# Three last weight groups walked one token half at a time, norms started before the next splits, modulation sums read first in a step

## The chip, the cores and the metric

The kernel runs on one NeuronCore of a Trainium2 chip. The metric is the time of one launch on the device in microseconds (us), the median of several runs. TensorE (PE) multiplies, VectorE (DVE) and ScalarE (ACT) work elementwise, GpSimd (POOL) does a few tiny powers, SyncE (SP) issues most DMAs. Everything is in fp32, with matrix products made of three products of rounded parts (below).

## The reference

All matrices have 256 tokens (two halves of 128 rows) and D = 2048 features. Cut to what matters here:

```
x = x + rmsnorm(y @ w_o[l], post_norm_g[l])          # end of each of two layers of block one
# block two, once:
sh1, sc1, g1, sh2, sc2, g2 = split(silu(c) @ w_mod + b_mod)   # w_mod is 2048 x 12288, one row vector c
h = rms_norm(x, g0) * (1 + sc1) + sh1
y = real(fft2(h in 8 groups of 256 features)) @ fnet_w_out    # over tokens and features
x = x + g1 * rms_norm(y, n1)
h = rms_norm(x, n2) * (1 + sc2) + sh2
x = x + g2 * rms_norm(square(relu(h @ w_mlp_in)) @ w_mlp_out, n3)
```

A layer of block one is: rmsnorm, one wide projection (latents, keys, a short gated convolution, memory queries, gates), two low-rank up-projections, attention of 8 heads with rotary positions, memory attention of 4 heads, a gate, and the output product with w_o.

## The kernel before

**Steps.** The whole program is a list of 576 steps. A step is half of a 1 MB unit of weights: two or so k-tiles of 128 x 512. SP loads units into a ring of four (`raw`), ACT writes the rounded high part of a step's weights (`split_hi`, L349, into a ring of four `whi`), DVE writes the rest in place (`split_lo`, L356, `wlo`), and PE makes three products per tile: activations high x weights high, high x low, low x high. Eight steps make a group (sixteen for the memory product, two in the up-projections), which fills two or four PSUM banks. Steps 0 to 287 are the two layers (144 each; the last 32 of a layer are w_o in four groups), 288 to 319 the product after the Fourier mix (four groups), 320 to 575 the MLP in four quarters of 64 steps (32 in, 32 out). The last groups of the three stages are thus steps 280 to 287, 312 to 319 and 568 to 575.

**Order.** Every engine walks the same list in its own instruction stream; nothing is reordered. ACT and DVE run `AHEAD = 3` steps ahead: in their iteration s they first split step s+3 and then do whatever else stands at s. `split_hi(s)` waits for the unit and for `half_used >= s-3`, which PE raises at the end of each step. SP loads unit u once unit u-4 is used up.

**w_mod.** The row vector times w_mod is made beside all this on DVE: 192 units of 128 x 1024 (`modacc`, L895), each at a step that a table names; 16 of them make a chunk, after which PE sums over partitions at a step of the same table (`mod_sums`, eight products with ones into one PSUM column, behind a wait for DVE), and DVE adds the eight columns to `modT` (`mod_added`, in the next iteration). Some PE work in that PSUM bank waits for that addition (`sums_read`).

**Ends of stages.** At the end of a stage, before the next one can begin, for both token halves: ACT squares the last group's outputs with a sum over the row (L590), DVE scales them into `otok` (L844), adds the four partial sums (L881), POOL adds eps and takes the power -0.5 (L549, L551), DVE adds to X (`residual`, L870, 2048 wide), ACT squares the new X (L583), POOL again. Then, after the layers, DVE scales the tables of the Fourier mix by the token's factor (`csx`, L1114) and PE multiplies X with them (64 products, all eight banks, here called the AB products) and then mixes within feature groups (64 more). Before the MLP, PE transposes the 16 feature tiles of X (L1439, two per bank) and a tile of the factors (`xrot`, L1450); ACT copies the factors (`mrow`, L806); then for each feature tile DVE multiplies (`x2_value`, L1163), ACT rounds (`x2_round`, L810) and DVE takes the rest (`x2_rest`, L1168): a pair of tiles feeds one MLP step. The first MLP group writes the four banks in which X tiles 0 to 7 lie, and so waits for their eight values. At the end of the MLP the same chain leads to the stores.

**Opening.** ACT waits for the first memory tiles, then loads its function table, rounds memory tiles (L601) and splits weights; DVE makes the rotary angles first (L852 to L860); step 7 waits for a tile made of the memory norm's factors (`mrot`, L1059), and ACT squares X at step 5.

## Time and profile before

| | |
|---|---|
| median of 3 runs | 1779.96 us (1779.45 to 1781.57) |
| the profiled execution | 1779.79 us, its span 1778.0 us |
| busy: PE, DVE, ACT, POOL | 1707.7, 1169.4, 833.7, 22.4 us |
| mean granted TensorE clock | 0.987 |

The span runs from the first to the last instruction. Times in the trace count from the span's start. PEclk is the granted share of TensorE's 2.4 GHz, so that 0.50 is 1.2 GHz.

### The profile page before, as it was taken

The numbers are of one execution on the slowest core, as the hardware profiler recorded it, in microseconds if no ns is written. First come the engines' busy times: TensorE is split into PE (matmuls) and PEld (weight loads), VectorE is DVE, ScalarE is ACT, GpSimd is POOL, SyncE is SP. The second block draws the span as 40 slices with busy tenths as digits, with TensorE's granted clock in tenths as the row PEclk, the third lists the DMA queues.
The fourth block names the chain that finished last, engine by engine and source line by source line (L and its number), as shares of the span: only waits on it lengthen the run. The fifth ranks groups of instructions, "written<-read, shape, count | busy, mean of one in ns | idle before, by whom it ended". The sixth has DMA issues, their size and how long they took to land.

```text
span 1778.0 us, 24585 instructions
## 1 busy us (share of the span) xinstructions
PE 1707.7 (96%) x10182; PEld 1526.7 (86%) x10182; DVE 1169.4 (66%) x1243; ACT 833.7 (47%) x1134; POOL 22.4 (1%) x35
## 2 busy tenths in 40 slices
PE   5999999999999999999979969999999999999997
PEld 5899999988889999998878858888888888888885
DVE  6677756687777866677748868644774455445554
ACT  5556545444655645544444444433443344334442
POOL 0010000000100000000000000000000000000000
PEclk9999999999999999999989989999999999999999
DMA  7587656698667857688837828656875555566553
GB/s 267 180 314 282 238 180 242 219 344 311 213 219 272 316 188 248 208 297 283 302 107 264 318 93 316 193 182 194 298 248 190 189 189 189 190 213 190 189 190 118
DMA packets 184927, 408.29 MB, mean 230 GB/s; under 512 B 8912, under 2 KB 21488, under 8 KB 184048
## 3 DMA queue, kind: packets, MB, share of 16 engines
q1 hardware_dynamic: 183808, 406.40, 66.6%
q8 instruction: 81, 1.33, 0.3%
q10 hardware_dynamic: 1008, 0.32, 0.1%
q14 instruction: 30, 0.25, 0.0%
HBM read 404.58 MB, written 2.11 MB: 229 GB/s over the span
## 4 chain that ended last, share of the span: by engine, by line
PE 89%; DVE 4%; DMA 4%; ACT 1%; issue 1%; POOL 0%; SPq 0%; DVEq 0%; ACTq 0%; POOLq 0%
PE banks L360 88%; DMA modw<-in_w_mod 3%; DVE modacc L895 1%; DVE wlo L356 1%; PE banks L1313 1%; DVE X L870 1%; DMA ropev<-in_rope_c 0%; ACT junk L583 0%; PE banks L1276 0%; ACT whi L349 0%; POOL sc L551 0%; DVE otok L844 0%; ACT junk L590 0%; DVE X L1233 0%; DVE sqr L1211 0%
## 5 line engine op out<-in xcount | busy, mean ns | idle before, releaser
L356 DVE TENSOR_TENSOR wlo<-raw,whi 128x1024 fp32r<-128x1024 f32 (+3 forms) x576 | 682.7, 1191 | 484.7 <-ACT whi L349 483.3
L349 ACT ACTIVATE whi<-raw 128x1024 fp32r<-128x1024 f32 (+3 forms) x576 | 590.5, 1031 | 735.7 <-PE banks L360 693.9
L360 PE MATMUL banks<-H,whi 128*128 128x256 f32 (+1 forms) x3072 | 744.4, 326 | 12.7 <-DVE vtmp L1163 7.7
L360 PE MATMUL banks<-H,wlo 128*128 128x256 f32 x2048 | 579.5, 283 | 0.0
L360 PEld LDWEIGHTS banks<-H,whi 128*128 128x128 f32 x3072 | 516.1, 191 | 63.2 <-DVE vtmp L1163 8.0
L360 PE MATMUL banks<-whi,Y 128*128 128x512 f32 x1536 | 475.6, 390 | 0.0
L360 PEld LDWEIGHTS banks<-H,wlo 128*128 128x128 f32 x2048 | 391.5, 191 | 0.1
L360 PEld LDWEIGHTS banks<-whi,Y 128*128 128x128 f32 x1536 | 288.5, 188 | 59.9
L360 PE MATMUL banks<-wlo,Y 128*128 128x512 f32 x768 | 299.3, 390 | 0.0
L895 DVE SCALAR_TENSOR_TENSOR modacc<-modw,cv,modacc 128x1024 f32<-128x1024 f32 x180 | 230.2, 1279 | 25.2 <-DMA modw<-in_w_mod 24.9
L360 PEld LDWEIGHTS banks<-wlo,Y 128*128 128x128 f32 x768 | 144.3, 188 | 29.5
L360 PE MATMUL banks<-whi,H 128*128 128x512 f32 (+1 forms) x512 | 149.8, 374 | 0.0
L360 PEld LDWEIGHTS banks<-whi,H 128*128 128x128 f32 x512 | 94.8, 190 | 15.0
L360 PE MATMUL banks<-wlo,H 128*128 128x512 f32 (+1 forms) x256 | 95.3, 372 | 0.0
L360 PEld LDWEIGHTS banks<-wlo,H 128*128 128x128 f32 x256 | 48.7, 190 | 7.4
L360 PE MATMUL banks<-memh,whi 128*128 128x256 f32 x128 | 38.2, 298 | 16.5 <-DVE wlo L356 16.5
L724 ACT ACTIVATE prob<-banks,sc 128x256 f32<-128x256 f32 x48 | 22.3, 470 | 55.0 <-DVE sc L1030 55.0
L833 ACT ACTIVATE Y<-sqr 128x1024 fp32r<-128x1024 f32 x16 | 17.0, 1062 | 52.5 <-DVE sqr L1211 52.5
L360 PEld LDWEIGHTS banks<-memh,whi 128*128 128x128 f32 x128 | 25.7, 201 | 17.0 <-issue 16.9
L360 PE MATMUL banks<-memh,wlo 128*128 128x256 f32 x128 | 37.3, 292 | 0.0
L360 PE MATMUL banks<-meml,whi 128*128 128x256 f32 x128 | 37.3, 292 | 0.0
L767 ACT ACTIVATE prob<-prob,sc 128x256 f32<-128x256 f32 x48 | 21.8, 502 | 22.2 <-DVE sc L1034 22.0
(183 smaller groups left out, 1223.3 us busy)
## 6 DMA issues: line engine op xcount, KB each, us to landing
modw<-in_w_mod SPq DMA_DIRECT2D x192, 512.0 KB, 6.2
raw<-in_w_in SPq DMA_DIRECT2D x72, 1024.0 KB, 5.2
raw<-in_w_mlp_in SPq DMA_DIRECT2D x64, 1024.0 KB, 5.2
raw<-in_w_mlp_out SPq DMA_DIRECT2D x64, 1024.0 KB, 5.0
raw<-in_w_o SPq DMA_DIRECT2D x32, 1024.0 KB, 5.3
raw<-in_w_fnet SPq DMA_DIRECT2D x16, 1024.0 KB, 5.2
raw<-in_w_mv SPq DMA_DIRECT2D x8, 1024.0 KB, 5.4
raw<-in_w_mk SPq DMA_DIRECT2D x7, 1024.0 KB, 5.4
```

The lines of the kernel that those rows point to most:

```text
L349: nc.scalar.activation(whi[step % HIR][:, 0:n], raw[u % RAW][:, (step % 2) * n:(step % 2) * n + n], ACT.Copy).then_inc(hi_ready, 1)
L356: nc.vector.tensor_tensor(wlo[u % RAW][:, part], raw[u % RAW][:, part], whi[step % HIR][:, 0:n].bitcast(F32), ALU.subtract).then_inc(lo_re ...
L360: return nc.tensor.matmul(o, a, b, start=start, stop=stop, skip_group_check=True)
L724: w = nc.scalar.activation(prob[:, b, t, :], M[b][:, t * SEQ:(t + 1) * SEQ], ACT.Exp, scale=scale, bias=sc[:, NM + 2 * b + t:NM + 2 * b + ...
L767: w = nc.scalar.activation(prob[:, b, t, :], prob[:, b, t, :], ACT.Copy, scale=sc[:, RINV + 2 * b + t:RINV + 2 * b + t + 1])
L833: nc.scalar.activation(Yhi[:, 4 * j:4 * j + 4, :], sqr[:, :, :], ACT.Copy).then_inc(m_hi, 1)
L870: nc.vector.scalar_tensor_tensor(X[:, t, :], otok[:, t, :], sc[:, OR + t:OR + t + 1], X[:, t, :], ALU.mult, ALU.add).then_inc(x_new, 1)
L895: nc.vector.scalar_tensor_tensor(modacc[:, :], modw[j % MRING][:, :], co, modacc[:, :], ALU.mult, ALU.add).then_inc(mod_used, 1)
L1313: i = nc.tensor.transpose(M[2][:, kt * SEQ + t * P:kt * SEQ + (t + 1) * P], prob[:, b, t, kt * P:(kt + 1) * P], ident[:, :])
```

## The change

The three last groups are done by token half: PE walks the eight steps for tokens 0 to 127 and then the same eight for tokens 128 to 255. `half_used` rises in the second walk only, so all eight steps' weights are held; the high parts of the first four go to `early` tiles in activation space that is free by then, and `free_after` and `stage_end` say what the splits wait for and where they stop. The stage's end is written per token half (`token_residual`, `token_norm`, `x_squares`, X in two halves of 1024), partial sums and eps come from one sum on DVE, and POOL only takes the power. The next stage's first three splits stand behind the norms. The AB products of the first half go in an order that ends with the banks still read. X tiles 8 to 15 go to banks 0 to 3 and are copied to SBUF (`xs`, 128 x 512 each, four of them) so that the first MLP group can start before their values are made. The gate row of the Fourier stage is made at steps 258 to 265 and sent by ACT. The table for w_mod skips every seventh step where it skipped every fifth, ends earlier, and its additions to `modT` come ahead of the split in an iteration. In the opening ACT's table is loaded ahead of the first wait, the angles move to step 18, memory tiles are asked for one unit later, and POOL takes the memory norm before that of X.

```diff
+BY_TOKEN = (FN_H - 8, ML_H - 8, END_H - 8)
+def free_after(step):
+    late = any(s + 4 <= step < s + 8 for s in BY_TOKEN)
+    return step - (2 if late else 1) * HIR + 1
+def stage_end(step):
+    return min(s + 8 for s in BY_TOKEN if step < s + 8)
...
         for s in range(18, 139):
-            if s not in HEAVY and s % 5:
+            if s not in HEAVY and s % 7 and l * LH + s < BY_TOKEN[0] - 3:
                 yield l * LH + s
...
+        early = [at(f"early{i}", [P, 4, 1024], kb, F32R) for i, kb in enumerate((0, 32, 0))]
...
             if step >= HIR:
-                act.wait_ge(half_used, step - HIR + 1)
+                act.wait_ge(half_used, free_after(step))
...
-                            if l == 0 and i < 3:
-                                load_memx(i + 1)
+                            if l == 0 and 1 <= i < 4:
+                                load_memx(i)
...
+            act.wait_ge(ones_set, 1)
+            act.wait_ge(pow_set, 4)
+            nc.scalar.activation(junk[:, 0:8], ones[:, :], ACT.Copy)
             act.wait_ge(small_in, 16)
...
             for t in range(MT):
-                act.wait_ge(x_new, 2 * DEPTH - 1 + t)
-                square(t, 2 * DEPTH + t + 1)
+                token_end(0, t)
+                row_square(acc[acc_of(NG - 1)][:, t * 512:(t + 1) * 512], 3, t)
+                x_squares(0, t)
+            for s in range(AHEAD):
+                split_hi(act, FN_H + s)
...
+            act.wait_ge(x2_T, 2)
+            x2_saved(0)
+            x2_saved(1)
+            act.wait_ge(x2_row, MT)
+            nc.scalar.activation(mrow[:, :], x2_place(KT - 1), ACT.Copy).then_inc(x2_rowed, 1)
...
                 for s in range(LH):
-                    split_lo(dve, base + s + AHEAD)
                     mod_added(base + s)
+                    if base + s + AHEAD < stage_end(base + s):
+                        split_lo(dve, base + s + AHEAD)
...
+            def by_token(stage, ps, act_in):
+                for t in range(MT):
+                    for i in range(8):
+                        step = BY_TOKEN[stage] + i
+                        if t == 0:
+                            pe.wait_ge(lo_ready, step + 1)
+                        w = tm_half(step, ps, act_in, 2 * i, 2, i == 0, i == 7, 512, [t])
+                        if t:
+                            w.then_inc(half_used, 1)
+                        elif i == 7:
+                            w.then_inc(token_done, 1)
...
-                for g in range(KT // 2):
+                for g in (0, 1, 4, 5, 6, 7, 2, 3) if t == 0 else range(KT // 2):
+                    if t == 0 and g in (2, 3):
+                        pe.wait_ge(row_out, g - 1)
...
                             if q:
                                 pe.wait_ge(acc_dve, DVE1 + 4 * (q - 1) + 2 * n + 2)
+                            elif n == 0:
+                                pe.wait_ge(x2_out, 4)
                             else:
-                                pe.wait_ge(x2_val, 8 * n + 8)
+                                pe.wait_ge(x2_val, 8)
```

The first place is VectorE's stream from the last splits of the second layer to the scaled Fourier tables; `raw_51` to `raw_54` are the four weight slots, `whi_59` to `whi_62` the four high-part slots. Before:

```order
L356 TENSOR_TENSOR wlo_56<-raw_52,whi_61 128x1024
L844 TENSOR_TENSOR otok<-banks,post 128x512 x2
L881 TENSOR_REDUCE sc<-sc 128x2
L844 TENSOR_TENSOR R<-modT,ngs 128x16
L1106 SCALAR_TENSOR_TENSOR A_123<-modT,ngs 128x16
L1107 TENSOR_SCALAR S_124<-modT 128x16
L870 SCALAR_TENSOR_TENSOR X<-otok,sc,X 128x2048 x2
L1114 TENSOR_SCALAR csx<-cs,sc 128x512 x2
```

And of the change, same engine and place:

```order
L385 TENSOR_TENSOR wlo_58<-raw_54,whi_62 128x1024
L961 TENSOR_REDUCE sc<-sc 128x1
L926 TENSOR_TENSOR otok<-banks,post 128x512
L966 SCALAR_TENSOR_TENSOR X<-otok,sc,X 128x1024 x2
L972 TENSOR_REDUCE sc<-sc 128x1
L1215 TENSOR_SCALAR csx<-cs,sc 128x512
L961 TENSOR_REDUCE sc<-sc 128x1
L926 TENSOR_TENSOR otok<-banks,post 128x512
L966 SCALAR_TENSOR_TENSOR X<-otok,sc,X 128x1024 x2
L972 TENSOR_REDUCE sc<-sc 128x1
L1215 TENSOR_SCALAR csx<-cs,sc 128x512
L385 TENSOR_TENSOR wlo_55<-raw_51,whi_59 128x1024
```

The chain now stands once per token half, and the next stage's splits moved from ahead of it to behind it.

The second place is ScalarE's stream at the entry of the MLP. Before, with the three splits already done ahead of it:

```order
L349 ACTIVATE whi_61<-raw_52 128x1024
L590 ACTIVATE junk,sc<-banks 128x512 x2
L583 ACTIVATE junk,sc<-X 128x2048 x2
L806 ACTIVATE mrow<-banks 128x256
L810 ACTIVATE H<-vtmp,modT 128x256 x6
L349 ACTIVATE whi_62<-raw_52 128x1024
```

And of the change:

```order
L607 ACTIVATE junk,sc<-banks 128x512
L378 ACTIVATE whi_59<-raw_51 128x1024
L378 ACTIVATE whi_60<-raw_51 128x1024
L618 ACTIVATE junk,sc<-X 128x1024 x2
L870 ACTIVATE xs<-banks 128x512 x2
L876 ACTIVATE mrow<-banks 128x256
L870 ACTIVATE xs<-banks 128x512 x2
L884 ACTIVATE H<-vtmp,modT 128x256 x2
L378 ACTIVATE whi_61<-raw_52 128x1024
L884 ACTIVATE H<-vtmp,modT 128x256 x4
```

Two splits and four copies of X tiles now stand between the last square and the first rounding, and only one pair of tiles is rounded before the third split.

The third place is VectorE's stream around the second sum of w_mod in the first layer (`modT`). Before, in the iteration of step 77:

```order
L356 TENSOR_TENSOR wlo_58<-raw_54,whi_62 128x1024
L356 TENSOR_TENSOR wlo_55<-raw_51,whi_59 128x1024
L844 TENSOR_TENSOR modT<-banks,modT 128x8
L1027 TENSOR_REDUCE sc<-banks 128x2
L1030 TENSOR_SCALAR sc<-sc 128x2
L892 TENSOR_SCALAR modacc<-modw_114,cv 128x1024
```

And of the change, in the iteration of step 74:

```order
L385 TENSOR_TENSOR wlo_57<-raw_53,whi_59 128x1024
L926 TENSOR_TENSOR modT<-banks,modT 128x8
L385 TENSOR_TENSOR wlo_57<-raw_53,whi_60 128x1024
L1132 TENSOR_REDUCE sc<-banks 128x2
L1135 TENSOR_SCALAR sc<-sc 128x2
L994 TENSOR_SCALAR modacc<-modw_114,cv 128x1024
```

The addition moved from behind the split of the same iteration to ahead of it. In the table the sums stand at steps 41, 73, 98, 120, 165, 193, 220, 246, 270, 302, 357 and 421 where they stood at 45, 76, 103, 129, 175, 205, 233, 262, 292, 312, 357 and 421.

## Rows read from the trace of the kernel before

**Rows 1.** The page: busy time and share of the span by engine.

```profile
PE 1707.7 (96%) x10182; PEld 1526.7 (86%) x10182; DVE 1169.4 (66%) x1243; ACT 833.7 (47%) x1134; POOL 22.4 (1%) x35
```

**Rows 2.** PE's waits: for whom, us in total, times, longest.

```profile
PE banks L360 <- DVE wlo L356: 21.5, 6, 16.2
PE banks L360 <- DVE modT L844: 5.3, 2, 2.6
```

**Rows 3.** Windows: length, busy us of each engine, clock, DMA share, GB/s.

```profile
873.44:895.21 21.77, 21.77 (x97) 17.70 (x95) 13.40 (x12) 9.63 (x12) 0.00 (x0) 1.00 0.73 241
895.21:904.58 9.37, 0.27 (x2) 0.12 (x2) 6.71 (x9) 4.88 (x8) 1.66 (x4) 0.70 0.66 237
904.58:921.13 16.55, 16.55 (x128) 16.55 (x129) 1.46 (x7) 6.37 (x16) 0.74 (x2) 0.86 0.18 66
1026.35:1047.06 20.71, 5.99 (x36) 5.31 (x35) 13.65 (x23) 9.74 (x17) 1.78 (x4) 0.72 0.16 51
1765.78:1778.00 12.22, 0.00 (x0) 0.00 (x0) 7.55 (x8) 1.33 (x4) 0.88 (x2) 0.64 0.43 172
```

**Rows 4.** The last w_o unit: its issue, and the DMA view's time to landing.

```profile
873.48 0.38 SPq L330 DMA_DIRECT2D raw<-in_w_o  x1
raw<-in_w_o SPq DMA_DIRECT2D x1, 1024.0 KB, 5.1
```

**Rows 5.** Timeline behind the second layer: start, length, engine, line, what.

```profile
895.24 0.60 ACT L590 ACTIVATE junk<-banks 128x512 bf16<-128x512 f32 x1 [1.60 <-PE banks L360]
897.80 0.69 POOL L551 TENSOR_TENSOR sc<-sc 128x2 f32<-128x2 f32 x1
898.52 4.61 DVE L870 SCALAR_TENSOR_TENSOR X<-otok,sc,X 128x2048 f32<-128x2048 f32 x2 [0.85 <-POOL sc L551]
900.91 1.91 ACT L583 ACTIVATE junk<-X 128x2048 bf16<-128x2048 f32 x1 [2.73 <-DVE X L870]
903.95 0.49 DVE L1114 TENSOR_SCALAR csx<-cs,sc 128x512 f32<-128x512 f32 x1 [0.81 <-POOL sc L551]
```

**Rows 6.** Timeline into the MLP.

```profile
1038.46 0.38 ACT L806 ACTIVATE mrow<-banks 128x256 f32<-128x256 f32 x1 [2.21 <-PE banks L1450]
1039.39 0.91 ACT L810 ACTIVATE H<-vtmp,modT 128x256 fp32r<-128x256 f32 x2 [0.55 <-DVE vtmp L1163]
1057.28 1.23 DVE L356 TENSOR_TENSOR wlo<-raw,whi 128x1024 fp32r<-128x1024 f32 x1 [0.46 <-ACT whi L349]
1060.83 1.23 DVE L356 TENSOR_TENSOR wlo<-raw,whi 128x1024 fp32r<-128x1024 f32 x1 [0.46 <-ACT whi L349]
```

**Rows 7.** The last four writes of X, from the timeline's end.

```profile
1769.74 4.87 DVE L1233 SCALAR_TENSOR_TENSOR X<-fin,sc,X 128x1024 f32<-128x1024 f32 x4 [1.15 <-POOL sc L551]
```

**Rows 8.** A wait at a sum of w_mod, then windows.

```profile
545.66 1.02 PE L360 MATMUL banks<-ones,modacc 128*128 128x1 f32 x8 [1.88 <-DVE modacc L895]
250.37:253.78 3.41, 3.41 (x12) 2.87 (x11) 0.65 (x1) 0.13 (x1) 0.00 (x0) 0.50 0.00 0
547.33:550.74 3.41, 3.41 (x15) 3.41 (x15) 2.02 (x2) 0.00 (x0) 0.00 (x0) 0.50 0.07 19
405.00:410.00 5.00, 5.00 (x24) 4.14 (x23) 1.44 (x2) 2.01 (x2) 0.00 (x0) 1.00 1.04 397
```

**Rows 9.** Timeline of the opening.

```profile
8.14 1.28 ACT L601 ACT_TABLE_LOAD   x1 [8.14 <-DMA memx<-in_memt]
33.00 1.06 ACT L349 ACTIVATE whi<-raw 128x1024 fp32r<-128x1024 f32 x1 [1.01 <-PE banks L360]
38.96 2.00 ACT L349 ACTIVATE whi<-raw 128x1024 fp32r<-128x1024 f32 x2 [0.17 <-ACT junk L583]
40.18 1.64 POOL L551 TENSOR_TENSOR sc<-sc 128x2 f32<-128x2 f32 x1
42.39 0.69 PE L1265 MATMUL banks<-ident,mrot 128*128 128x128 f32 x2 [3.43 <-DVE mrot L1059]
```

**Rows 10.** Window around the longest wait in the MLP.

```profile
1305.00:1320.00 15.00, 12.98 (x74) 11.16 (x74) 11.05 (x10) 7.98 (x8) 0.00 (x0) 1.00 0.62 211
```

More of the change, by code:

```diff
@@ L132, in mod_slots @@
         for s in range(18, 139):
-            if s not in HEAVY and s % 5:
+            if s not in HEAVY and s % 7 and l * LH + s < BY_TOKEN[0] - 3:
                 yield l * LH + s
-    for s in range(1, 30):
+    for s in range(1, 22):
         if s % 8:
@@ L146, in may_sum @@
         s = step % LH
-        return 18 <= s < LH - 1 and s not in M3_BUSY and s - 1 not in M3_BUSY
+        return 18 <= s < LH - 1 and s not in M3_BUSY and s - 1 not in M3_BUSY and step < BY_TOKEN[0] - 1
     if step < ML_H:
-        return step - FN_H <= 31
+        return step < BY_TOKEN[1] - 1
     return 37 <= (step - ML_H) % 64 <= 44
@@ L249, in build_program @@
         mix = at("mix", [P, 2, 2, SEQ], 52)
-        rowb = [at(f"rowb{i}", [P, D], A + 44 + 8 * i) for i in range(2)]
+        rowb = at("rowb", [P, D], A + 52)
         cross = at("cross", [P, CT, SEQ], A + 4)
@@ L341, in slot, with hi_part @@
             return raw[u % RAW][:, 0:nk * n].rearrange("p (k n) -> p k n", k=nk)
+        def hi_part(step, n):
+            for i, s in enumerate(BY_TOKEN):
+                if s <= step < s + 4:
+                    return early[i][:, step - s, 0:n]
+            return whi[step % HIR][:, 0:n]
         def split_hi(act, step):
@@ L363, in halves @@
             n = nk * width
[L364 removed]
+            hi = hi_part(step, n).rearrange("p (k n) -> p k n", n=width)
             lo = wlo[step // 2 % RAW][:, (step % 2) * n:(step % 2) * n + n].rearrange("p (k n) -> p k n", n=width)
@@ L379, in fm_half, with tm_half @@
             return w
-        def tm_half(step, ps, act_in, k0, nk, first, last, width):
+        def tm_half(step, ps, act_in, k0, nk, first, last, width, tokens=range(MT)):
             hi, lo = halves(step, width, nk)
@@ L386, in tm_half @@
                 k = k0 + kk
-                for t in range(MT):
+                for t in tokens:
                     o = ps[:, t * 512:t * 512 + width]
@@ L756, in _ @@
                         ended(act, l, ENDED[s])
+                    if l == DEPTH - 1 and s == GATE_ROW[2]:
+                        act.wait_ge(r_T, 1)
+                        nc.scalar.activation(rows[0][:, :], M[0][0:KT, 0:P], ACT.Copy).then_inc(rows_ready, 1)
+                        write_row(0)
+                    if l == DEPTH - 1 and s == GATE_ROW[3]:
+                        spread_row(0)
                     for i in range(4):
@@ L790, in _ @@
                     nc.scalar.activation(Hhi[:, 2 * g - 4:2 * g - 2, :], mix[:, g % 2, :, :], ACT.Copy).then_inc(f_hi, 1)
-            for s in range(33):
-                if s < 32:
+            for s in range(32):
+                if FN_H + s + AHEAD < ML_H:
                     split_hi(act, FN_H + s + AHEAD)
@@ L811, in x2_round @@
                                      bias=modT[:, 3 * KT + f:3 * KT + f + 1]).then_inc(x2_hi, 1)
-            for f in range(2 * AHEAD):
+            for f in range(2):
+                x2_round(f)
+            split_hi(act, ML_H + 2)
+            for f in range(2, 2 * AHEAD):
                 x2_round(f)
@@ L836, in _ @@
                         nc.scalar.activation(rows[1][:, :], M[3][0:KT, 0:P], ACT.Copy).then_inc(rows_ready, 1)
+                        write_row(1)
+                    if q == 2 and s == 43:
+                        spread_row(1)
                     if q == 3 and s in (41, 49, 57):
                         whole_squares(s // 8 - 5)
-            whole_squares(3)
+            for t in range(MT):
+                act.wait_ge(row_out, 4 + t + 1)
+                row_square(otok[:, t, 1536:], 3, t)
         @block.vector
@@ L1006, in _ @@
                         residual(l - 1)
-                    if l == 0 and s == 11:
+                    if l == 0 and s == 18:
+                        angles()
+                    if l == 0 and s == 21:
                         dve.wait_ge(sin_ready, 2)
@@ L1190, in _ @@
                 base = ML_H + 64 * q
-                for s in range(65):
+                for s in range(65 if q < 3 else 64):
+                    if s < 64:
+                        mod_added(base + s)
                     if s < 64 and base + s + AHEAD < END_H:
@@ L1255, in _ @@
                 base = l * LH
-                for s in range(LH):
+                for s in range(LH if l + 1 < DEPTH else LH - 8):
                     if l == 0 and s == MSUM_AT:
@@ L1421, in _ @@
                 w.then_inc(f_ps, 1)
-            for s in range(32):
+            for s in range(24):
                 n = s // 8
@@ L1456, in _ @@
             for q in range(4):
-                for s in range(64):
+                for s in range(64 if q < 3 else 56):
                     n = s // 8
@@ L1492, in _ @@
                     w.then_inc(half_used, 1)
+            pe.wait_ge(m_pre, 16)
+            by_token(2, pair[3], (Yhi, Ylo))
 def kernel(**inputs):
```

313 lines of the change are left out of this document (189 added, 124 removed).

## The prediction

> **What bounds the kernel now.** I read the page first, then PE's waits, then windows around each wait, then the timelines in them. TensorE is busy 1707.7 us, 96% of the span of 1778.0 [rows 1], so the kernel is bound by PE wherever PE is not made to wait, and the question of each edit is which PE wait it shortens. The 70.3 us in which PE has nothing to do are few and large: 16.2 until its first product [rows 2], 9.1 between the second layer and the Fourier mix, 14.7 at the entry of the MLP, 12.2 behind the last product [rows 3]; together 52.2. The other 18 are waits of 0.4 to 3.4 us, of which two, 5.3 together, are for the addition to `modT` [rows 2]. Beside the idle time stands the clock: after a pause the granted clock is at its lower level, 1.2 GHz, for a while. The AB window shows it: 16.55 us at a mean of 0.86, which is 14.2 us of work at 2.4 GHz [rows 3].
>
> **The change part by part.** All positions below are counted from T, the end of the last product of a stage's last group.
>
> *The walks by token.* The number of products is the same, so the walks add nothing to PE by themselves. Eight steps take 21.77 us [rows 3], so one step of one token half takes 21.77/16 = 1.36, and the first walk asks for weights twice as fast. Step index 6 is wanted 8.2 us into the group, index 7 at 9.5. Their unit is issued at the group's start and lands 5.1 later [rows 4]; a high part takes 1.0 (two in 2.00 [rows 9]), a low part 1.23 [rows 6]: index 6 is ready at about 5.1 + 1.0 + 1.2 = 7.4, index 7 at 8.7 (VectorE is the slower, 1.23 after 7.4). That is 0.8 before each is wanted, so the walks of the w_o and Fourier stages cost 0. In the MLP's last group more stands in the way: in iteration 57 ScalarE squares the third output group (about 1.5: four of 0.6 less overlap [rows 5] and their readouts) behind VectorE's addition (1.2, ready about 3.5 in), so high part 5 ends at 6.2, low part 5 at 7.4 where 6.8 is wanted, and `final_gain` (1.3) pushes low part 6 to 9.9 where 8.8 is wanted after the first wait grew to 0.6. Together 1.6 us lost.
>
> *Into the Fourier mix.* Before, the AB products start 9.37 after T and end 25.9 after T [rows 3]. Now the first half's tables are long ready (its chain lay under the second walk of 10.9 us), and PE multiplies the 32 products of half one, 7.1, right after T. Half two needs: square 0.75 with its readout, sum 0.15, power 0.69, so X may be written from 1.9; two halves of X of 1024 columns, 1.28 and 1.2 (four took 4.87 [rows 7]), to 4.4; its second square, about 1.2 with readout (between 0.60 for 512 and 1.91 for 2048 columns), to 5.6; sum, power, table 0.49 [rows 5]: 7.0 after T. So PE waits 0 to 0.5, and ends the AB products 14.4 after T, with the clock never let down. Gain 25.9 - 14.4 = 11.5, less the gate row's transposition that went elsewhere (0.27): **11.2**. The three splits behind the norms (3 us of ScalarE to 8.7 after T) end about when the first AB bank is complete, 8.1.
>
> *Into the MLP.* Before, the first step starts 20.7 after T [rows 3]. Now, by the same rows: X written 4.4 after T, squares done 5.6, sum, power and `xrot` 6.9, PE's factor tile 7.2, `mrow` (0.38 [rows 6]) 7.6. ScalarE then owes two copies of 512 columns, 0.60 each as the square of that width takes [rows 5], to 8.9 (the first two lie before `mrow`), the rounding of two tiles 0.91 [rows 6] to 9.9, and VectorE's rest ends at 10.3. PE starts step 0 at 10.4. But now VectorE sets the pace: a split and a pair of X tiles take it 1060.83 - 1057.28 = 3.55 us per step [rows 6], PE 2.81 (16 of the 74 products in 12.98 [rows 10]). Pairs are ready at 10.3, 14.0, 15.8, 19.4 and then every 3.55, the eighth at 33.6. Step 7 started 43.0 after T before (20.7, one slow step, six of 2.8); it now starts at 33.6. Gain **9.4**, not 10.3. The low clock in step 0 hides behind these waits.
>
> *The end.* Before, 12.2 from T [rows 3]. Now only token half two is left: addition of 512 columns 0.7, square with readout to 1.55, sum, power to 2.55, X in 1.28 and 1.2 to 5.1, then the last store as before, 3.4 (4.87 after 1769.74 [rows 7] leaves 1778.0 - 1774.6). 8.5 in all: gain 3.7, less the 1.6 above: **2.1**.
>
> *The sums of w_mod.* In step 77 of the first layer (and in 90 of the second) PE waits 2.6 for `modT` [rows 2], because VectorE's addition stands behind a split that waits for the step just before. With the addition ahead of it both such waits (5.3 [rows 2]) go. Behind the first of them PE worked 3.41 us at a clock of 0.50, and so again at 547.33 behind a wait of 1.88 for the unit two steps earlier [rows 8]: 1.7 lost each. The sum at step 175 has moved to 165 and no longer follows a run of short steps, so its 1.88 goes too. Gone: 5.3 + 1.9 + 3.4 = 10.6. Given back: the first sum now stands at 41, where the unit of step 39 ends late behind the key rotations, about 0.7; the short up-projection steps carry one or two units more, about 0.6 of new wait at step 56; the other moved sums about 1.3. Net **8**, between 4 and 10.6. The angles (ten small instructions on VectorE, under 4 us) now lie at step 18, where splits run ahead by more than that: 0; without that lead they would cost PE up to 4.
>
> *The opening.* The table load of 1.28 [rows 9] and the angles leave the path to the first product, which comes near 12 instead of 16.15. But then ScalarE's split for step 8 waits for a unit whose load is queued behind X in a DMA that is already saturated; from its place in the queue it lands at about 31.8 as before, an estimate, and that split started at 33.0 [rows 9]. The squares of X behind it, which end at 38.8 [rows 9], move by only 1.2, and `mrot` by 1.8, its wait for POOL (a power of 1.64 at 40.18 [rows 9]) gone. PE arrives early and waits: its 3.43 [rows 9] becomes about 6.6, and more low clock follows. Gain **1**, between 0 and 4.
>
> The sum: 11.2 + 9.4 + 2.1 + 8 + 1 = 31.7. The profiled execution took 1779.79 (span 1778.0 and 1.8 around it), 0.2 under the median of 1779.96, so 1779.9 - 31.7 = **1748.2 us**.
>
> Where the trace gives two prices: POOL's power took 0.69 with VectorE waiting and 1.64 beside it [rows 5, 9]. I take 0.69, as VectorE waits at that point in the new chains too; at 1.64 the two chains before the mix and at the end are each 1 us longer, which goes into the range. The Trainium skill ("GPSIMD Engine Reference", Specifications) says that GpSimd shares its way into SBUF with VectorE and is in contention with instructions that read two tensors from SBUF. By that rule the powers that run beside the final gain (two SBUF tensors) would be slow, and the sum would be 1 us less; the trace's slow power at 40.18 agrees.
>
> **The rivals.** (a) *The first walks starve.* What speaks for it: only 0.8 us is spare, and the landing of 5.1 [rows 4] is one unit's, and is longer where the queue is full. If each landing is 2 late and a low clock of 3.4 follows, each walk loses 1.2 + 1.7, the three 9: 1757. Against it: no w_mod unit is loaded there now. (b) *w_mod units come late*, since six of seven steps now carry 1 MB of loads, 1.05 MB in 2.72 us or 385 GB/s, while the fullest 5 us that I looked at moved 397 [rows 8]. The additions then stall VectorE and, behind it, splits. With splits three steps ahead PE feels it only at sums and in the short steps; at 2 us for five of them 1758. (c) *The other side: the clock.* In the first walks PE may wait a little before each step, and if the granted clock stays at 1.2 GHz through all three, 3 x 10.9 = 32.7 us are added, 1781, and through the second walks too 1813. It decides against the change once more than 31.7 us of extra time is spent at the lower level. Against it: in 1305 to 1320 PE was idle for 2.02 and the clock stayed at 1.00 [rows 10]; for it: behind a wait of 1.88 it stood at 0.50 [rows 8]. The Trainium skill ("TensorE: Matmul & The Clock Gate", A second HAM failure mode) reports a kernel in which short pauses between groups of products made the clock go back and forth; by that rule (c) is what the walks would do. The trace bears it out only for single waits of about 2 us. (d) *The opening pays in full*: the split of step 8 does not wait for the load, and 4.2 are gained: 1745. (e) *Nothing happens*, since something else than the chains holds PE: the windows show none.
>
> **How the numbers follow.** Forecast case 0.68 (1742 to 1754 by its own bounds: sums 4 to 10.6, opening 0 to 4, powers 2, end 1.6); (a) 0.10, (b) 0.10, (c) 0.03, (d) 0.07, (e) 0.02. The range takes in (a), (b) and (d): **1740 to 1759**. 0.2%, some 3.6 us, is about what a measurement of this kernel tells from no change. Faster 0.95, same 0.02, slower 0.03.
>
> **What would show it.** The AB products begin within 0.3 us of T and the mean clock over them is 1.00; the first MLP step starts 10 to 11 after T and the next seven come at VectorE's pace of 3.55; the span ends 8 to 9 after the last product; no wait for `modT` is left; the first product is near 12 and the wait for `mrot` is longer than 3.43. Wrong would be: waits for `wlo` in the first walks of more than 1 us each, a PE wait for a sum of over 1 us in the second layer's gates, a clock under 1.00 in a walk.

## The result, and the profile after

The changed kernel takes 1749.9 us (median of 4 runs, 1748.48 to 1755.02), the kernel before, beside it, 1779.7 (4 runs, 1777.67 to 1781.57); the ratio is 0.9831, 95% interval 0.9811 to 0.9852. The profiled execution has a span of 1746.6 us at a mean granted clock of 0.994, 31.4 less than the 1778.0 of before.

The busy times, from the page of the changed kernel:

```profile
span 1746.6 us, 24610 instructions
PE 1702.8 (97%) x10182; PEld 1521.4 (87%) x10182; DVE 1168.2 (67%) x1255; ACT 835.4 (48%) x1147; POOL 25.8 (1%) x34
```

PE is busy 4.9 us less than in [rows 1] with the same products. Some 4.1 of that is clock: 15.2 us of its work lay at the lower clock where 23.4 did, and half of such time is lost. The rest is mostly a pace in the MLP's first quarter, to which I come under `after_again`. PE's waits, total, times and longest:

```profile
PE banks L389 <- DVE wlo L385: 21.1, 7, 12.2
PE banks L1384 <- DVE mrot L1164: 5.1, 1, 5.1
PE banks L389 <- issue: 2.0, 1, 2.0
...
PE banks L389 <- DVE H L1275: 1.4, 3, 0.5
...
PE banks L389 <- DVE modacc L997: 1.3, 2, 0.7
PE banks L1579 <- DVE X L966: 1.0, 1, 1.0
```

No wait for `modT` is left (5.3 in [rows 2]) and none for the tables `csx`; the first product comes at 12.2 instead of 16.2; the wait for `mrot` has grown from 3.43 [rows 9] to 5.1. The windows that answer to [rows 3], on the changed kernel: both walks of the last w_o group together, the AB products, the mixing, from T to the first MLP product, the first eight MLP steps, and the end.

```profile
869.20:891.10 21.90, 21.90 (x98) 18.16 (x97) 11.06 (x14) 9.22 (x15) 1.10 (x2) 1.00 0.46 154
891.17:905.61 14.44, 14.44 (x131) 14.43 (x130) 8.08 (x15) 11.60 (x23) 1.08 (x2) 1.00 0.62 239
905.61:919.67 14.06, 14.06 (x129) 14.06 (x128) 8.42 (x25) 7.61 (x14) 0.00 (x0) 1.00 0.00 1
1008.66:1018.66 10.00, 4.97 (x35) 3.62 (x34) 7.61 (x12) 8.85 (x16) 1.08 (x2) 0.98 0.49 183
1018.66:1044.63 25.97, 24.55 (x128) 20.68 (x129) 21.55 (x37) 14.28 (x23) 0.00 (x0) 0.94 0.39 122
1738.41:1746.60 8.19, 0.16 (x1) 0.00 (x0) 4.02 (x5) 0.72 (x2) 0.55 (x1) 0.72 0.32 128
```

The walks of the first window run without a pause at a clock of 1.00 (so do those of the Fourier stage; the MLP's has the two waits below), the AB products follow at once and end 14.4 after T, where they ended 25.9 after it [rows 3]. The table below counts every stretch from T in both kernels. T is taken as the start of the last product plus 0.23, the time from product to product, which in the kernel before is some 0.2 earlier than in [rows 3].

| stretch | before | after | gain |
|---|---|---|---|
| start to step 9 (opening) | 51.92 | 50.79 | 1.1 |
| step 9 to T of w_o, and the Fourier groups (sums) | 843.13 + 90.85 | 840.39 + 88.99 | 4.6 |
| T of w_o to the first Fourier step (AB and mixing) | 40.30 | 28.50 | 11.8 |
| T of Fourier to MLP step 8 | 46.02 | 35.97 | 10.1 |
| MLP step 8 to the last product | 693.40 | 693.78 | -0.4 |
| last product to the end | 12.40 | 8.19 | 4.2 |

The gains make 31.4. The rest of the MLP is 0.4 longer: two waits in its last group's first walk cost 1.6, and the pace in its first quarter gave 1.3. PE's list has these two waits as 1.05 only, in part because it counts a product as busy for 0.39 where the next one starts after 0.23; by the starts of the same products, those behind the two waits come 1.6 later than in `pairs_and_end`, where the waits are gone. Below, "counted on the same products" means this comparison.

### The profile page after: what moved, and what is told of

It is laid out like the page before. It is cut to its first block, busy times and chain, and to the rows that moved or that the text cites. A ratio compares the mean times of both kernels' runs of the same rounds, so it can differ in the third digit from the quotient of the medians.

```text
span 1746.6 us, 24610 instructions
## 1 busy us (share of the span) xinstructions
PE 1702.8 (97%) x10182; PEld 1521.4 (87%) x10182; DVE 1168.2 (67%) x1255; ACT 835.4 (48%) x1147; POOL 25.8 (1%) x34
## 4 chain that ended last, share of the span: by engine, by line
PE 88%; DVE 4%; DMA 4%; ACT 2%; issue 2%; POOL 0%; DVEq 0%; SPq 0%; ACTq 0%; POOLq 0%
PE banks L389 87%; DMA modw<-in_w_mod 3%; DVE modacc L997 1%; ACT whi L378 1%; DVE wlo L385 1%; PE banks L1432 1%; DMA raw<-in_w_in 0%; DMA gs<-in_small 0%; PE banks L1395 0%; ACT H L884 0%; ACT junk L601 0%; DVE vtmp L1270 0%; DVE X L966 0%; DVE sqr L1321 0%; DVE pre L926 0%
## 5 line engine op out<-in xcount | busy, mean ns | idle before, releaser
L385 DVE TENSOR_TENSOR wlo<-raw,whi 128x1024 fp32r<-128x1024 f32 (+3 forms) x564 | 667.2, 1189 | 447.2 <-ACT whi L378 445.7
L378 ACT ACTIVATE whi<-raw 128x1024 fp32r<-128x1024 f32 (+3 forms) x564 | 576.5, 1030 | 678.9 <-PE banks L389 626.8
L389 PE MATMUL banks<-whi,Y 128*128 128x512 f32 x1472 | 456.9, 390 | 1.1 <-DVE wlo L385 1.1
L389 PEld LDWEIGHTS banks<-whi,Y 128*128 128x128 f32 x1472 | 276.3, 188 | 59.6 <-DVE wlo L385 1.9
L389 PE MATMUL banks<-whi,H 128*128 128x512 f32 (+1 forms) x480 | 138.7, 369 | 0.0
L389 PEld LDWEIGHTS banks<-whi,H 128*128 128x128 f32 x480 | 87.7, 188 | 13.7
L389 PE MATMUL banks<-memh,whi 128*128 128x256 f32 x128 | 38.2, 298 | 12.3 <-DVE wlo L385 12.2
L569 POOL TENSOR_TENSOR sc<-sc 128x1 f32<-128x1 f32 (+1 forms) x18 | 16.0, 887 | 1525.3 <-DVE sc L1348 724.8
L389 PEld LDWEIGHTS banks<-memh,whi 128*128 128x128 f32 x128 | 25.9, 202 | 12.9 <-issue 12.7
```

The costliest lines, as they stand in the source:

```text
L378: nc.scalar.activation(hi_part(step, n), raw[u % RAW][:, (step % 2) * n:(step % 2) * n + n], ACT.Copy).then_inc(hi_ready, 1)
L385: nc.vector.tensor_tensor(wlo[u % RAW][:, part], raw[u % RAW][:, part], hi_part(step, n).bitcast(F32), ALU.subtract).then_inc(lo_ready, 1)
L389: return nc.tensor.matmul(o, a, b, start=start, stop=stop, skip_group_check=True)
L569: nc.gpsimd.tensor_tensor(sc[:, r0:r0 + n], sc[:, m0:m0 + n], sc[:, POW:POW + n], ALU.pow).then_inc(done, 1)
```

## The experiments

Spans are of one profiled execution each; medians are of 4 to 6 runs and ratios are to the kernel before in the same session. The medians of before in the four sessions were 1781.6, 1784.3, 1782.3 and 1781.1.

**The order of the addition to `modT`.** In the changed kernel, and the reverse in the kernel before (at all three places where the pair of lines stands):

```diff
-                    mod_added(base + s)
                     if base + s + AHEAD < stage_end(base + s):
                         split_lo(dve, base + s + AHEAD)
+                    mod_added(base + s)
```

> The changed kernel, with the addition to modT put behind the split of its iteration again, as it stood before. Three sums are read by a product in the very next step (first layer 73 and 98, second layer 76). My theory, that the addition stood behind a split which waits for the step just before: three waits for modT of about 2.6 us come back, 7.8 us, and up to 1.7 of low clock behind each, so a span of 1754.4 to 1759.5 where the changed kernel has 1746.6. Rival, that the new places of the sums and not the order took the waits away: span within 1.5 us of 1746.6 and no wait for modT.

> The kernel before with this one part of the change: the addition to modT ahead of the split of its iteration. My theory: both waits for modT (5.3 us) go, and with them the low clock of 3.41 us behind the first (1.7 us); span 1778.0 - 7.0 = 1771.0, median near 1772.9. Rival: the reader of the sum waits for something else that is late anyway (the probabilities of the head), gain under 2 us.

`sums_behind`: median 1764.2, ratio 0.9908 (0.9892 to 0.9923), span 1760.7. Its list of waits has the row that was forecast, and no other wait grew by more than 0.6; the span lies 1.2 above my range:

```profile
PE banks L389 <- DVE modT L926: 8.2, 3, 2.9
```

Counted on the same products, the three steps that wait make TensorE 4.8, 2.9 and 2.9 later, 10.5 in all: the 8.2, low clock behind the first, and some 0.2 with each wait that the list doesn't show. Of the other 3.6, 1.4 arose before 116 us and the rest in stalls, low clock and the MLP's pace elsewhere, of which below. `before_sums_first`: median 1774.1, ratio 0.9961 (0.9948 to 0.9974), span 1772.9; no wait for `modT`, 5.1 gained where 7.0 was expected. The ratio gives 6.9 (0.0039 of 1781.6). Counted on the same products, the two waits and the clock behind the first gave 4.5 and 2.9. The order is the cause; the new places of the sums are not. The low stretch at 250 is gone, but another stood at 621.0 to 624.4, which the kernel before did not show, and the one behind the wait of 1.9 at 541.5 was 6.8 long where it had been 3.4.

**The walk by token.** Only PE's order in the last groups is put back:

```diff
-                for t in range(MT):
-                    for i in range(8):
+                for i in range(8):
+                    for t in range(MT):
```

> The changed kernel, but in the last groups TensorE takes both halves of the tokens step by step, as it did before; all else (the chain of norms by halves, ahead of the splits) stays. My theory, that the second walk hides the first half's chain: into the Fourier mix the first half's table is ready 6.3 us after T, not long before, the second's at 13, so the AB products end 21 to 22 after T where they ended 14.5 (6.5 to 8 lost); into the MLP the second half's row is about 5.6 later; at the end the second half waits for the first, 4.3 lost, less 1.05 of waits in the first walk that go. Span 1762, between 1760 and 1765. Rival, that handling norms by halves and ahead of splits is worth most of it and the walk little: under 5 us lost.

Median 1768.3, ratio 0.9931 (0.9918 to 0.9945), span 1765.5. AB waited for the first table, and then worked at a mean clock of 0.90 (PE's timeline and a window):

```profile
901.18 9.01 PE L389 MATMUL banks<-csx,X 128*128 128x129 f32 x65 [5.54 <-DVE csx L1215]
...
901.18:917.00 15.82, 15.82 (x128) 15.82 (x129) 8.02 (x14) 10.92 (x21) 1.08 (x2) 0.90 0.10 39
```

Into the mix 7.3 are lost (5.5 of wait, 1.8 of clock), into the MLP 4.2, at the end 3.5, and the 1.6 of the waits in the first walk go: 13.4 of the 18.9, and the span lies 0.5 above my range. The other 5.5 are low stretches elsewhere (604, 843) and a longer stall at step 28 of the MLP's second quarter, to which I come below. I had the second table as what AB waits for; it was ready before the first half's products were done, so only the first table counts.

**The norms ahead of the splits**, put back before the mix alone, on ScalarE and in the same way on VectorE:

```diff
+            for s in range(AHEAD):
+                split_hi(act, FN_H + s)
             for t in range(MT):
                 token_end(0, t)
...
-            for s in range(AHEAD):
-                split_hi(act, FN_H + s)
```

> The changed kernel with ScalarE's and VectorE's splits for the first three steps of the Fourier stage ahead of the norms again (the stage before the mix alone). They wait for weights that the second walk gives back 9.5 us into it, so the first half's chain starts about when the second walk ends instead of 10 before. My theory: first table 6.5 to 7 after T, second table 12.5 to 13, AB products end near 20.8 instead of 14.5, 6 to 7 us lost and up to 1.7 of low clock; span 1753 to 1755. Rival, that only the second half's norm counts, for which the order does not matter as the splits are done by T: under 1.5 us lost.

Median 1764.0, ratio 0.9883 (0.9869 to 0.9896), span 1763.2: 11.8 lost into the mix, where I expected 6 to 8.7 with the clock, and all that the change had gained there; the other 4.8 of the 16.6 arose elsewhere, mostly in low stretches at 605 and 844. ScalarE's timeline, PE's, and the window over AB show why:

```profile
893.38 2.01 ACT L378 ACTIVATE whi<-raw 128x1024 fp32r<-128x1024 f32 x2 [12.74 <-DMA raw<-in_w_fnet]
896.04 1.06 ACT L378 ACTIVATE whi<-raw 128x1024 fp32r<-128x1024 f32 x1 [0.65 <-DMA raw<-in_w_fnet]
897.00 0.58 ACT L607 ACTIVATE junk<-banks 128x512 bf16<-128x512 f32 x1
...
904.66 1.20 PE L389 MATMUL banks<-csx,X 128*128 128x129 f32 x4 [9.43 <-DVE csx L1217]
...
904.66:921.32 16.66, 16.66 (x130) 16.66 (x131) 4.61 (x11) 8.16 (x18) 1.08 (x2) 0.87 0.01 1
```

I had counted until the weights are given back; the unit must then still be issued and land. The third high part was begun 1.0 after T (895.06) where I had it done 0.4 before T, the first square stood behind it, AB began 9.6 after T, and after this pause the clock was low, which cost 2.2 more (16.66 where 14.44 stands above). A split that waits for a load holds everything behind it on its engine.

**The tiles of X moved out of the banks**, put back:

```diff
-            return bank((f // 2 + 4) % 8)[:, f % 2 * SEQ:(f % 2 + 1) * SEQ]
+            return bank(f // 2)[:, f % 2 * SEQ:(f % 2 + 1) * SEQ]
...
-                            elif n == 0:
-                                pe.wait_ge(x2_out, 4)
-                            else:
-                                pe.wait_ge(x2_val, 8)
+                            else:
+                                pe.wait_ge(x2_val, 8 * n + 8)
```

> The changed kernel without the copies xs: all 16 tiles of X stay in banks at entry of the MLP, and the first group waits for eight values as it did before. My theory, that VectorE sets the pace there (3.55 us a step): the first product comes 7.5 to 8 us later than 10.0 after T, but step 8 only 2 to 4 later than 35.97, as the steps behind it catch up with VectorE; span 1749 to 1751. Rival, that each microsecond of the first product's start is worth a microsecond: step 8 also 7.5 to 8 later, span 1754.

Median 1759.1, ratio 0.9859 (0.9846 to 0.9873), span 1757.6. The first product came 17.6 after T instead of 10.0, as expected, but step 8 came 5.9 later, between my 2 to 4 and the rival's 7.5 to 8. The span is 11.0 longer because another 4.9 arose before T, in stalls and low clock where the edit changes nothing. VectorE's pace binds only from the sixth MLP step on; before that PE works at its own 2.8 in both kernels, so there are 1.7 to catch up with, not 4.

**The opening.** The block that makes `mrot` goes ahead of its iteration's split on VectorE:

```diff
                     mod_added(base + s)
+                    if l == 0 and s == MROW_AT - 1:
+                        dve.wait_ge(mem_rstd, 1)
...
                     if base + s + AHEAD < stage_end(base + s):
                         split_lo(dve, base + s + AHEAD)
```

> The changed kernel with one block moved in VectorE's program: the two operations on mrot in iteration 6 stand ahead of that iteration's split, whose high part ScalarE makes only behind the squares of X. My theory of why the opening gained 1.1 where TensorE began 3.9 earlier: mrot stood behind that split. Its factor has been there since 35.9, so mrot is done at 36.4, TensorE's wait for it falls from 5.06 to 1 or so, the first transposition of X comes near 45.5 instead of 50.38, and the span is 1741.0 to 1742.5 (4.1 to 5.6 less, the more if the low clock behind the wait goes). Rival, that the transfers and ScalarE's squares hold the opening: the wait for xn grows by what the wait for mrot loses, gain under 1.5 us.

In the opening this came true in part. PE's timeline:

```profile
36.89 0.44 PE L1384 MATMUL banks<-ident,mrot 128*128 128x128 f32 x2 [2.21 <-DVE mrot L1105]
45.80 0.55 PE L1395 MATMUL banks<-ident,xn 128*128 128x128 f32 x2 [2.85 <-DVE xn L1175]
```

Step 9 came 4.4 and step 18 still 3.1 earlier. But the span was 1751.3, where I had 1741.0 to 1742.5, 4.7 more than the changed kernel's, and the median 1749.5, ratio 0.9824 (0.9807 to 0.9842), no more than 0.0007 better. The windows behind three stalls that both kernels have, first of the changed kernel at two of them, then of `mrot_first` at three:

```profile
603.60:607.00 3.40, 3.38 (x28) 3.40 (x29) 2.99 (x3) 2.06 (x3) 0.00 (x0) 1.00 0.99 364
842.10:845.50 3.40, 3.40 (x17) 2.81 (x17) 0.41 (x2) 0.31 (x1) 0.00 (x0) 1.00 0.97 377
```

```profile
602.50:605.90 3.40, 3.40 (x19) 3.40 (x18) 2.70 (x3) 2.96 (x4) 0.00 (x0) 0.52 1.01 372
841.40:844.80 3.40, 3.40 (x10) 2.69 (x9) 0.08 (x2) 0.00 (x0) 0.00 (x0) 0.51 0.88 340
1284.50:1288.00 3.50, 3.46 (x12) 2.95 (x13) 3.50 (x4) 1.38 (x2) 0.00 (x0) 0.58 0.39 149
```

Counted on the same products, the three low stretches cost 4.6, the stall at step 28 was 1.2 longer, some 0.9 of the gain was lost again before 116 us, and 1.3 is the MLP's pace, shown next.

**The changed kernel once more**, to tell whether these belong to a kernel or to an execution.

> The changed kernel once more. In mrot_first the opening was 3.1 us shorter and yet the span 4.7 longer: behind three stalls that both kernels have (steps 56 and 126 of the second layer, step 28 of the MLP's second quarter) the granted clock fell for 3.4 us each in mrot_first and not in the profile of the changed kernel. My theory: whether it falls behind such a stall differs from execution to execution. Then this profile has the same stalls in the same places, but not the same low windows, and its span differs from 1746.6 by a multiple of about 1.7. Rival: the low windows belong to the kernel (its exact timing); then both profiles show the same ones, and mrot_first is truly slower.

Median 1751.7 (5 runs, 1747.2 to 1754.43), ratio 0.9815 (0.9798 to 0.9831), span 1749.1. The stalls stood where they were; the clock did not. The stretch at 141 ran at 0.50 in the first profile and at 1.00 here, the one at 603 the other way round:

```profile
141.12:144.54 3.42, 3.42 (x31) 3.42 (x30) 0.81 (x1) 1.65 (x4) 0.00 (x0) 1.00 0.19 32
603.50:606.90 3.40, 3.40 (x18) 3.40 (x18) 3.01 (x3) 2.32 (x3) 0.00 (x0) 0.51 0.98 365
```

So the low clock behind a short stall differs from execution to execution. Half of 3.4 us is 1.7; counted on the same products each cost 1.5 to 1.7. In the eight profiles with the changed kernel's table it followed the stall at step 56 of the first layer 8 times, at step 41 7 times, at step 56 of the second layer 7 times, at its step 126 5 times, and at step 28 of the MLP's second quarter once, though that stall was 0.9 to 3.3 long. Both profiles of the changed kernel drew two such stretches, `mrot_first` five and most others four.

As both drew two, my multiple of 1.7 should have been nought, and the spans differ by 2.5. A second thing differed: the same 360 products of the MLP's first quarter took 62.4 us in the first profile and 63.6 here, both without a pause and at a clock of 1.00 (windows of the changed kernel's first profile and of `after_again`):

```profile
1045.90:1108.30 62.40, 62.40 (x361) 55.02 (x360) 49.72 (x42) 28.54 (x29) 0.00 (x0) 1.00 0.80 274
1047.18:1110.78 63.60, 63.60 (x361) 55.18 (x360) 50.01 (x42) 28.50 (x29) 0.00 (x0) 1.00 0.79 269
```

Of the 14 profiles 9 had the longer time, the kernel before among them, and 5 the shorter; over the whole quarter it is 1.3. What sets it is not known. The other 1.2 are longer stalls, half of it before 116 us.

**The table of w_mod.** Fewer units in the short steps, more behind them, and no sum at 40 to 44; then, in `table_mlp`, also the MLP's units spread:

```diff
-            if s not in HEAVY and s % 7 and l * LH + s < BY_TOKEN[0] - 3:
+            if s not in HEAVY and s not in (50, 52, 54) and (s % 7 or s > 57) and l * LH + s < BY_TOKEN[0] - 3:
...
-        return 18 <= s < LH - 1 and s not in M3_BUSY and
+        return 18 <= s < LH - 1 and not 40 <= s <= 44 and s not in M3_BUSY and
```

```diff
-        for s in range(10, 36):
+        for s in range(10, 42, 2):
             yield ML_H + 64 * q + s
```

> The changed kernel with another table of w_mod units: none at 50, 52 and 54 of a layer, no gap at every seventh step behind 57, and no sum at 40 to 44, so the first sum stands at 45. My theory, that the sums gained 4.6 where 8 was forecast because the new table made two stalls and the low clock behind each of them cost 1.7: the wait at 41 (0.68) and 1.3 of the 2.15 at step 56 go with both low windows (141 and 172), 4.5 to 5 us, and the 3.09 at step 56 of the second layer is halved; span 1741 to 1743. Rival, that VectorE is simply full here and the units moved behind 57 stall there: new waits for modacc or wlo, span within 1.5 of 1746.6.

> table_spread with one more line of the table: in the first two quarters of the MLP the 16 units of w_mod stand at every second step from 10 to 40 instead of at 16 steps in a row from 10. In all kernels so far TensorE waits 2.06 to 2.29 for a low part at step 28 of the second quarter. My theory, that 16 additions of 1.28 beside splits of 1.23 and the work of an output group leave VectorE late there: the wait goes, and with it the low clock that followed in table_spread (1.6); span 1738.3 to 1740.3 where table_spread has 1742.4. Rival, that this wait is a late transfer of weights and not VectorE: it stays or moves, span within 1 us of 1742.4.

`table_spread`: median 1743.1, ratio 0.9769 (0.9755 to 0.9782), span 1742.4. T of w_o comes 6.3 earlier: the waits at steps 41 and 56 are down from 0.68 and 2.15 to 0 and 0.38, and at step 56 of the second layer from 3.09 to 0.15. The two windows that were low in the changed kernel, here:

```profile
141.12:144.54 3.42, 3.42 (x31) 3.42 (x31) 2.38 (x5) 2.81 (x6) 0.00 (x0) 1.00 0.34 126
171.84:175.26 3.42, 3.42 (x30) 3.42 (x30) 2.69 (x4) 1.75 (x2) 0.00 (x0) 1.00 1.05 402
```

One new wait of about 1.1 for `modacc` (the sum at step 120) had a low stretch behind it. `table_mlp`: median 1737.5, ratio 0.9752 (0.9731 to 0.9774), span 1737.8; the stall at step 28 is gone and the low stretch behind it too. That is 3.9 of the 4.6 between the two spans. The rest is not the edit's: the wait at step 120 did not come this time (2.9 gained), the opening was 1.7 longer, and the MLP's pace was the slower one.

**Two more moves**: the values of a pair ahead of the split at entry of the MLP, and the third output group's squares and gain behind the last split.

```diff
+                    if pair_now:
+                        x2_value(2 * (s + AHEAD))
+                        x2_value(2 * (s + AHEAD) + 1)
                     if s < 64 and base + s + AHEAD < END_H:
                         split_lo(dve, base + s + AHEAD)
...
-                    if q == 3 and s in (42, 50, 58):
+                    if q == 3 and s in (42, 50, 62):
```

> The changed kernel with two moves. At entry of the MLP VectorE makes the two values of a pair ahead of the split of its iteration and their rests behind it; in the last quarter the squares and the gain of the third output group stand behind the last split. My theory, that the pace of 3.55 is the wait of VectorE for ScalarE and back (0.46 + 0.18 a step) put on a busy 2.9: the pace falls to TensorE's 2.8 to 2.9, the three waits for H (1.4) go, step 8 stands 34.5 after T instead of 35.97; and both waits for wlo in the last first walk (1.05) go. Span 1744.2, give or take 1.7 for each stall behind which the clock falls or does not. Rival, that VectorE's own work is the pace: step 8 stays at 36.0 after T.

Median 1748.1, ratio 0.9812 (0.9785 to 0.984): no difference from the changed kernel that the medians can tell; span 1746.6. The pace itself is settled by VectorE's timeline, first changed kernel, then this one:

```profile
1035.06 1.23 DVE L385 TENSOR_TENSOR wlo<-raw,whi 128x1024 fp32r<-128x1024 f32 x1 [0.46 <-ACT whi L378]
...
1037.26 0.89 DVE L1275 SCALAR_TENSOR_TENSOR H<-vtmp,modT,H 128x256 fp32r<-128x256 f32 x2 [0.18 <-ACT H L884]
1038.61 1.23 DVE L385 TENSOR_TENSOR wlo<-raw,whi 128x1024 fp32r<-128x1024 f32 x1 [0.46 <-ACT whi L378]
```

```profile
1030.39 1.22 DVE L385 TENSOR_TENSOR wlo<-raw,whi 128x1024 fp32r<-128x1024 f32 x1
1031.53 0.87 DVE L1275 SCALAR_TENSOR_TENSOR H<-vtmp,modT,H 128x256 fp32r<-128x256 f32 x2
1032.32 0.87 DVE L1270 SCALAR_TENSOR_TENSOR vtmp<-xs,A,mrow 128x256 f32<-128x256 f32 x2
1033.11 1.21 DVE L385 TENSOR_TENSOR wlo<-raw,whi 128x1024 fp32r<-128x1024 f32 x1
```

3.55 a step became 2.72; 0.6 of the 3.55 was waiting for ScalarE. Step 8 stands 35.0 after T, 0.9 better and not 1.4, since the first step now took 5.3 in place of 4.3 at the low clock. Both waits in the last first walk are gone (1.05 in the list, 1.6 counted on the same products). Four low stretches in the layers (140, 171, 604, 843), two more than in the changed kernel's profile, took the gain back in this execution.

**All of them**, with `free = step + 3` in place of `free = step + 2` in the table's plan; and then both halves of `xn` in iteration 6:

```diff
-X_N_AT = (7, 5)
+X_N_AT = (6, 5)
...
-                        if s == X_N_AT[l] + t:
+                        if s == X_N_AT[l] + l * t:
```

> All at once: table_mlp, mrot_first and pairs_and_end, and a sum three steps behind its last unit instead of two. Table_spread's span is 1742.4. From it go 3.1 in the opening (as mrot_first measured up to step 18), 2.3 and 1.6 of low clock at step 28, 1.4 at the entry of the MLP, 1.05 in the last walk, 1.1 and 1.6 of low clock at the sum of step 120: 1730.2, between 1728 and 1734. Rival, that the parts share their covers (an earlier TensorE meets the same transfers and ScalarE later): 1736 or more.

> all_moves (span 1730.3) with both halves of xn made in VectorE's iteration 6, behind its split, instead of in iterations 7 and 8 behind theirs. There TensorE waits 2.84 for xn and then works 2.8 at the low clock. My theory, that only the order on VectorE makes xn late: its factors are there at 39.05, xn ends near 42.9, TensorE's step 8 ends at 43.1, so the wait goes and step 9 starts near 43.9 instead of 46.72; span 1727.5, and 1726 if the low clock goes as well. Rival, that the rest of the opening follows VectorE anyway (its splits and rounded tiles are later by the 2.5 that xn takes from them): step 18 not earlier than 75.97, span within 1 us of 1730.3.

`all_moves`: median 1732.0, ratio 0.9717 (0.9697 to 0.9736), span 1730.3, where 1730.2 was expected. That it is so near is in part chance: more was gained in the layers and in the last walk than I had counted, and the MLP's pace was the slower one. `all_and_xn`: median 1726.8 (5 runs, 1726.04 to 1728.77), ratio 0.969 (0.9666 to 0.9714), span 1724.7, 5.6 less where 2.8 to 4.3 were expected. Of these 2.7 are left of the opening's gain at T of w_o; 1.7 are a shorter low stretch at the entry of the MLP and 1.3 its pace, neither of them the edit's. The kernel is faster than both kernels, and its longest waits are:

```profile
PE banks L389 <- DVE wlo L385: 13.2, 3, 12.2
PE banks L389 <- issue: 2.0, 1, 2.0
PE banks L1389 <- DVE mrot L1105: 1.9, 1, 1.9
...
```

## Why the prediction was right, and where its sum was off

The time was forecast at 1748.2 and is 1749.9; the forecast span of the profiled execution, 1778.0 - 31.7 = 1746.3, was in fact 1746.6. Three terms were too small (0.6, 0.7 and 0.5), one too large (3.4), and 1.3 came that the sum did not have, the pace of the MLP's first quarter; they nearly cancel. That the total fits to 0.3 is luck: with the slower pace, which 9 of 14 profiles had, it would have been 1.6 off.

*Into the Fourier mix*: 11.2 forecast, 11.8 measured (0.27 of it the gate row's transposition, which went elsewhere). Half two's table was done 6.9 after T (7.0) and AB never waited. Two runs show that both halves of the edit are needed: without the walk 7.3 are lost, with the splits ahead of the norms all 11.8. The walks' spare was 0.5 to 0.9 per step where I had 0.8.

*Into the MLP*: 9.4 forecast, 10.1 measured. First step 10.0 after T (10.4), step 7 at 33.1 (33.6). The pace of 3.55 was right; `pairs_and_end` adds that it was the hand-over between two engines and not their work.

*The end*: 2.1 forecast, 2.6 measured (4.2 less 1.6). The tail is 8.2 where I had 8.5, another 0.2 is the earlier T of the table, and the stalls in the last first walk cost the 1.6 that I had.

*The powers*: I took 0.69 and kept 1.64 as a bound. In all three ends they took 0.54 or 0.55, now for one value. POOL did slow down elsewhere, as here at the second layer's start, where VectorE read two tensors of SBUF for splits and `meml` beside it (POOL's timeline):

```profile
470.44 4.22 POOL L569 TENSOR_TENSOR sc<-sc 128x2 f32<-128x2 f32 x1
```

The Trainium skill ("GPSIMD Engine Reference", Specifications) has GpSimd share its way into SBUF with VectorE; I had weighed that it might cost 1 us at the end. The slow power above agrees. At the end the rule had nothing to act on: the last power began at 1740.33, when the final gain (to 1740.03) was over.

*The sums of w_mod*: 8 forecast, 4.6 measured, inside my 4 to 10.6. This is the term that was mis-sized: "Given back" named 0.7 at step 41, 0.6 at step 56 and 1.3 elsewhere, and no clock. Measured were 0.68 at 41, 1.3 more at 56 and 1.5 more at step 56 of the second layer, and a low stretch behind each of the first two (1.7 each), in the place of the two that went. Those take 6.9 from the 10.6, which leaves 3.7. Most of the other 0.9 is again what the list of waits leaves out: in `before_sums_first` a wait for `modT` listed as 2.63 cost 2.9 on the same products, and this stretch has five stalls where it had eight, an estimated 0.7. I had priced low clock as a gain where a stall went, and not as a cost where one came. `table_spread` shows it in one profile: with one wait gone and the other down to 0.38 the two stretches go. Rival (b) is borne out in small: in the short steps VectorE waits for late units, as its timeline of the changed kernel shows (the transfers ran at 394 GB/s there):

```profile
168.00 1.28 DVE L997 SCALAR_TENSOR_TENSOR modacc<-modw,cv,modacc 128x1024 f32<-128x1024 f32 x1 [1.83 <-DMA modw<-in_w_mod]
...
174.54 1.28 DVE L997 SCALAR_TENSOR_TENSOR modacc<-modw,cv,modacc 128x1024 f32<-128x1024 f32 x1 [1.57 <-DMA modw<-in_w_mod]
```

*The opening*: 1 forecast, 1.1 measured, for the right reason in the main (12.2 for the first product, the wait for `mrot` up to 5.1 where I had 6.6, and 6.8 us of low clock from 38.7 where there had been 3.4). What held it was sharper than my account of the load and the squares: `mrot` stood behind one split on VectorE, and `xn` behind two more. With both moved, step 18 comes 6.4 earlier.

*The rival of the other side, (c)*: all three walks of the changed kernel ran at 1.00. "A second HAM failure mode" in the Trainium skill ("TensorE: Matmul & The Clock Gate") speaks of a clock that goes back and forth with short pauses. The runs agree as to single stalls, of 0.5 to 3.2 us, but not each time; no run here paused within every group of a walk, so that case was not tried.

## What to carry to other kernels

Where a stage ends in a chain over tokens, finish half of the tokens early and put the chain ahead of anything on its engines that waits for a load: here leaving out the walk gave back 7.3 of the 11.8 into the mix, and leaving out the order all of it. When an instruction is late, look first at what stands before it in its own engine's program; four of the gains here were a move of a few lines. Price each stall that an edit brings with the low clock behind it, and judge a change of a few us by several executions and stretch by stretch, since one profile here drew two low stretches behind such stalls and another five.

## What was unexpected of the hardware

A stall of 0.7 us (step 41) was followed by some 3.4 us at a clock near 0.50 in 7 of 8 profiles; the one of 0.9 to 3.3 in the MLP's second quarter in 1 of 8; the stall at step 56 of the second layer (2.4 to 3.2) was followed by none in one profile, where it was 3.09 long, and by such a stretch in the seven others. I had expected the same program to show the same clock. That the same products can take 1.3 us longer at the same clock I had not expected either. Kernels with few stalls may also be steadier, which is not shown: the changed kernel's runs spread over 6.5 and 7.2 us, those of `table_spread`, `table_mlp` and `all_and_xn` over 2.1, 2.6 and 2.7, but those of `all_moves` over 4.9 and of `tiles_in_banks`, with all the stalls, over 3.2.
